# An encoder block: the attention's small sums moved from VectorE to GpSimd, and five orders changed

## The chip, the cores and the metric

One core of a Trainium2 chip runs the whole program in one launch. The metric is device time in microseconds, from a median over several executions. The engines are named as in the profile: PE (TensorE), DVE (VectorE), ACT (ScalarE), POOL (GpSimd) and SP, which only issues transfers.

## The reference, cut to what matters

An encoder layer on 1024 rows of 1024 columns, fp32: sliding-window attention and a two-way retention side by side, a cross-attention into 256 memory tokens, and a SwiGLU. Each ends in a normed addition to the stream. The part at which most of the change is made:

```
blk = jnp.arange(nb)[:, None, None]
...
valid = (jnp.abs(qpos - kpos) <= WINDOW) & (kpos >= 0) & (kpos < S)
s = jnp.where(valid, s, -jnp.inf)
sk = sink.astype(jnp.float32).reshape(ATTN_KV_HEADS, G)[None, :, :, None, None, None]
m = jnp.maximum(jnp.max(s, axis=-1, keepdims=True), sk)
p = jnp.exp(s - m)
p = p / (jnp.sum(p, axis=-1, keepdims=True) + jnp.exp(sk - m))
o = jnp.einsum('bhgnqk,bnkhd->bnqhgd', p.astype(v.dtype), vw)
```

So each row of scores has a maximum that takes in a learned sink logit, and a denominator that is the row's sum plus the sink's exponential.

## The kernel before, in words

Every engine has one instruction stream, written out by hand in its order; semaphores carry the dependencies. An engine does its instructions strictly in that order: one that waits holds up all behind it.

**Matrix products.** Each fp32 factor is split into a high and a low part, and `three()` (L1377 to L1379) does three matmuls for one product. For a weight piece of 128x512, SP loads it into one of four raw slots (`load`: it waits until the low part of the piece four places before is done), ACT rounds the high part, POOL subtracts for the low part, and PE multiplies. Low parts of activations are made by DVE from PSUM. Some products are done by a scheme of seven block products for eight; it needs sums of weight blocks. For the output projection, POOL makes these sums (L1156 to L1161, four rounds of four, 128x512 each) in the attention stage; SP loads a round's blocks, and stores the sums to a scratch in HBM.

**Attention, 248 to 341 us.** 16 steps, two (one per key/value head, four query heads each) for each of the 8 row blocks; I call the two a pair. In step s PE turns the exponentials (L1368), ACT and DVE copy them out (`copy_probs`, L2276 and L3190), and PE does the scores of step s + 2 (L1551) and the values of step s (L1589). DVE does `maxima(s + 2)`: four times the masking and the maximum (L3177), then the addition of the sink to the negated maxima (L3182, 128x4, both inputs in SBUF). ACT does the exponentials of step s + 1 and then the sink's (`sink_term`). In each second step DVE does `denominators(n)`: row sums plus sink exponentials (L3199, 128x8) and the reciprocal (L3201); then `values_out(n)`, which copies the turned values from PSUM (L3208, named junk_c) for PE to turn back. `attended(n)` (L3214) scales them by the reciprocal a step later. POOL's 16 sums for the output projection lie here, each round as soon as its blocks have landed.

**Cross-attention, about 500 to 760 us.** `quarter(q)` on PE is a quarter of the cross-attention's output product; its first begins when DVE has made eight low parts (L3551, semaphore `x_lo`). On ACT `q_round(n)` rounds the query's weight pieces, and `xo_round(n)` the output's 32 pieces; the last of these are mixed with the norms (`post(t)`, `pre(t)`) and with the high parts of turned rows (`row_high(t)`). POOL's low parts are L1255 and L1262.

**SwiGLU, from about 748 us.** `first_chunk(n)` is a product of the first block, four times three matmuls; behind each of the first four PE turns a row block (`turn_rows_h3`, eight transpositions), ACT rounds it (L2716) and DVE makes its low part (L3609). For the later blocks, c = 1 and on, ACT's loop mixes `weight_high(c + 1, j)` (rounding of the next block's weights, which POOL's weight sums L1284 precede), `gate_silu` and `bank_copy` (L2817).

Of the kernel before, what the change touches and what calls it, by code (L numbers as in the profile page):

```python
# [19 lines left out]
ALU = mybir.AluOpType  # L20
# [6 lines left out]
NT = S // P  # L27
# [205 lines left out]
def build(nc, x, mem, norm_mix_pre, norm_mix_post, w_in, attn_sink, attn_out_norm, ret_decay_fwd,  # L233
# [3 lines left out]
    with ExitStack() as ctx:  # L237
# [857 lines left out]
        def _(pool):  # L1095
# [54 lines left out]

            for k in range(RING):
                split(U_O, U_O, k, 512)
            for r in range(RING):
                a11, a12, a21, a22 = (o_stage(r, b) for b in range(4))
                pool.wait_ge(o_in[r % 2], O_IN + 64 * (r // 2 + 1))
                nc.gpsimd.tensor_tensor(a21, a21, a22, ALU.add).then_inc(o_summed, 1)  # L1156
                pool.wait_ge(o_summed, O_SUMMED + 4 * r + 1)
                nc.gpsimd.tensor_tensor(a11, a21, a11, ALU.subtract).then_inc(o_summed, 1)
                pool.wait_ge(o_summed, O_SUMMED + 4 * r + 2)
                nc.gpsimd.tensor_tensor(a12, a12, a11, ALU.subtract).then_inc(o_summed, 1)  # L1160
                nc.gpsimd.tensor_tensor(a22, a22, a11, ALU.subtract).then_inc(o_summed, 1)  # L1161

            pool.wait_ge(dk_v, 12)
            pool.wait_ge(sc_ready, NT * AH)
# [201 lines left out]
        def _(pe):  # L1366
# [581 lines left out]
            def quarter(q):  # L1948

                u = U_XO + q * NK  # L1950
                for k in range(NK):
                    if q == 2 and k >= RING:
                        turn_rows_h3(k - RING)
                    if q == 0 and k in (3, 4):
                        mem_turn(3 + k)
                    pe.wait_ge(w_split, u + k + 1)
                    for t in range(4):
                        if q == 1 and k == 0:
                            pe.wait_ge(x_lo, NK + RING + t + 1)
                        if q == 2 and k == 0:  # L1960
                            pe.wait_ge(xo_gain, t + 1)
                        c = slice((4 * (q // 2) + t) * P, (4 * (q // 2) + t + 1) * P)
                        last = three(ps[:, 4 * (q % 2) + t, :], t_hi[:, k, c], t_lo[:, k, c],
                                     w_hi[:, k % RING, :], w_lo[:, k % RING, :], k == 0, k == NK - 1)
                        if t == 3:
                            last.then_inc(w_used, 1)
                        elif k == NK - 1:
                            last.then_inc(tile_done, 1)

            pe.wait_ge(x_lo, NK)  # L1970
            pe.wait_ge(x_exp, XH * NT)
            quarter(0)
            mem_values(1)
# [4 lines left out]
            def first_chunk(n):  # L1978

                m, bank_no, first, high, low, c = (  # L1980
                    (0, 0, True, t_hi, t_lo, 0), (1, 0, False, t_hi, t_lo, 0), (2, 1, True, t_hi, t_lo, 0),
                    (3, 1, False, t_hi, t_lo, 0), (0, 2, True, t_hi, t_lo, 512), (2, 0, True, t_hi, t_lo, 512),
                    (1, 2, False, t_hi, t_lo, 512), (3, 0, False, t_hi, t_lo, 512))[n]
                if n < 4:
                    pe.wait_ge(g_lo, n + 1)
                if n == 0:
                    pe.wait_ge(h_dve, 8)
                    pe.wait_ge(xo_gain, 12)
                if n == 4:
                    pe.wait_ge(h_dve, 15)  # L1990
                if n == 5:
                    pe.wait_ge(c_act, 1)
                if n == 6:
                    pe.wait_ge(h_dve, 16)
                w_high, w_low = first_weights(m)
                for k in range(4):
                    w = slice(k * P, (k + 1) * P)
                    kk = 4 * (m % 2) + k
                    last = three(ps[:, bank_no, :], w_high[:, w], w_low[:, w], high[:, kk, c:c + 512], low[:, kk, c:c + 512],
                                 first and k == 0, not first and k == 3)  # L2000
                last.then_inc(g_prod, 1)
# [28 lines left out]
                                 first and k == 0, k == 3, not first)  # L2030
                last.then_inc(g_prod, 1)

            for n in range(4):
                first_chunk(n)
                turn_rows_h3(4 + n)
            first_chunk(4)
            for n in range(5, 8):
                first_chunk(n)
# [55 lines left out]
        def _(act):  # L2094
# [431 lines left out]
            for c in range(4):  # L2526
                if c == 2:
                    for i in range(4):
                        act.wait_ge(turned, TURNED_K + i + 1)
                        nc.scalar.activation(kM[:, 2 * i:2 * i + 2, :], bank(4 + i).rearrange("p (k m) -> p k m", k=2),  # L2530
                                             ACT.Copy).then_inc(act_ev, 1)
                    round_units(RING)
                if c == 3:
                    for n in range(3):
                        q_round(n)
                if c == 0:
                    act.wait_ge(o_joined, 12)
                for t in range(NM):
                    if t == 0:
                        act.wait_ge(tile_done, TILES["kv"] + c + 1)  # L2540
                    else:
                        act.wait_ge(w_used, U_KV + NK * (c + 1))
                    dst = kst if c < 2 else vM_hi
                    nc.scalar.activation(dst[:, t, (c % 2) * 512:(c % 2 + 1) * 512], bank(2 * (c % 2) + t),
                                         ACT.Copy).then_inc(act_ev, 1)
                if c == 3:
                    q_round(3)
                if c < 3:
                    for t in (2 * c, 2 * c + 1):
                        hi_parts(h2_turned(t), t_hi, t * P)  # L2550
                if c == 0:
                    round_units(2)
                    sums(("post", 4))
                    round_units(2)
                    sums(("post", 5))
                    round_units(RING)
                elif c == 1:
                    sums(("pre", 4), ("pre", 5), ("post", 6), ("post", 7))
                elif c == 2:
                    round_units(3)  # L2560
                    sums(("pre", 6))
                    round_units(1)
                    sums(("pre", 7))
                else:
                    round_units(RING)
# [210 lines left out]
            post(2)  # L2776
            pre(1)
            xo_round(21)
            post(3)
            pre(2)  # L2780
            xo_round(22)
            row_high(0)
            pre(3)
            xo_round(23)
            row_high(1)
            xo_round(24)
            xo_round(25)
            row_high(2)
            for n in range(26, 32):
                xo_round(n)  # L2790
            row_high(3)
            for t in range(4, NT):
# [56 lines left out]
            for c in range(1, NC - 1):  # L2849
                if c > 1:  # L2850
                    bank_copy(c, 1)
                    weight_high(c + 1, 0)
                weight_high(c + 1, 1)
                bank_copy(c, 2)
                if c == 1:
                    sum_high(6)
                    sum_high(7)
                if c > 1:
                    weight_high(c + 1, 2)
                gate_silu(c, 0)  # L2860
                bank_copy(c, 4)
                if c == 1:
                    weight_high(c + 1, 2)
                weight_high(c + 1, 3)
                weight_high(c + 1, 4)
                weight_high(c + 1, 5)
                gate_silu(c, 1)
                weight_high(c + 1, 6)
# [107 lines left out]
        def _(dve):  # L2976
# [190 lines left out]
            def maxima(s):  # L3167
# [3 lines left out]
                for j in range(G):  # L3171
# [3 lines left out]
                    if s >= 2:  # L3175
# [1 line left out]
                    nc.vector.tensor_tensor_reduce(sm[:, s % 2, j, 0:nk], bank(j, nk), band[:, off:off + nk],  # L3177
                                                   -A_SCALE, nsink[:, h:h + 1], ALU.add, ALU.min,
                                                   wnm[:, n, h:h + 1]).then_inc(w_max, 1)
                dve.wait_ge(w_max, G * (s + 1))  # L3180
                hs = slice(g * G, (g + 1) * G)
                nc.vector.tensor_tensor(wds[:, n, hs], sink[:, hs], wnm[:, n, hs], ALU.add).then_inc(w_small, 1)  # L3182

            def copy_probs(s, j):
                q = G * s + j
# [9 lines left out]
            dve.wait_ge(sink_turned, 1)  # L3195
            def denominators(n):

                dve.wait_ge(w_exp, 10 * (n + 1))
                nc.vector.tensor_tensor(wden[:, n, :], wrs[:, n, :], wes[:, n, :], ALU.add).then_inc(w_den, 1)  # L3199
                dve.wait_ge(w_den, 2 * n + 2)  # L3200
                nc.vector.reciprocal(wrd[:, n, :], wden[:, n, :]).then_inc(w_den, 1)  # L3201

# [20 lines left out]
            for s in range(steps):  # L3223
                n = s // AKV
                copy_probs(s, 1)
                copy_probs(s, 3)
                if s % AKV == 0 and n:
                    attended(n - 1)
                if s + 2 < steps:
                    maxima(s + 2)  # L3230
                if s % AKV == AKV - 1:
                    denominators(n)
                    values_out(n)

            def decay_scores(h):
                for b in range(2):
# [630 lines left out]
```

## Time and profile before

| what | value |
|---|---|
| median of 3 runs | 1394.73 us (1394.01 to 1396.04) |
| profiled execution, its own time | 1395.81 us |
| its span, first to last instruction | 1393.3 us |
| PE busy | 1366.7 us, 98% |
| POOL busy, DVE busy, ACT busy | 876.7, 879.2, 671.6 us |
| mean granted clock of PE | 0.999 |

The profiled execution is one of several. Its span leaves out 2.5 us before the first and behind the last instruction. PE is the engine with hardly any idle time, 27 us in all, so an edit's worth is read from what PE waits for.

### The profile page before, as it was taken

How to read it: one execution, taken by the hardware profiler on the slowest of the kernel's cores; microseconds unless marked ns; L12 is line 12 of the kernel's file. 1: busy time of each engine (PE TensorE's matmuls, PEld its weight loads, DVE VectorE, ACT ScalarE, POOL GpSimd, SP SyncE). 2: the span in 40 equal slices, each digit the busy share in tenths (PEclk: the TensorE clock that was granted, in tenths of full speed). 3: DMA queues.
4: the chain of work that ended last, by engine and by line, in shares of the span. 5: the costliest groups of instructions: out<-in, count | busy, mean ns of one | idle time of the engine just before them, and what ended most of it. 6: DMA issues, size and time to landing. Idle time of an engine off the chain costs nothing.

```text
span 1393.3 us, 18814 instructions
## 1 busy us (share of the span) xinstructions
PE 1366.7 (98%) x6644; PEld 1135.0 (81%) x6644; DVE 879.2 (63%) x1254; ACT 671.6 (48%) x1357; POOL 876.7 (63%) x600
## 2 busy tenths in 40 slices
PE   7999999999999999999999999999999999999998
PEld 7998888756988888888878888888888888878886
DVE  5799997887887888764267732333332333474868
ACT  6432233666686774354376433333333333544454
POOL 1697256421868976511354787777777774799653
PEclk9999999999999999999999999999999999999999
DMA  5676133540027555301535233233333325933354
GB/s 204 211 246 212 46 91 106 159 145 1 1 61 278 176 184 167 102 31 33 187 101 209 62 114 106 98 114 114 106 106 104 100 84 178 370 93 99 110 206 153
DMA packets 137756, 183.56 MB, mean 132 GB/s; under 512 B 10304, under 2 KB 82368, under 8 KB 137664
## 3 DMA queue, kind: packets, MB, share of 16 engines
q1 hardware_dynamic: 135360, 177.25, 38.8%
q10 hardware_dynamic: 2304, 5.13, 1.0%
q8 instruction: 53, 0.87, 0.3%
q14 instruction: 39, 0.32, 0.1%
HBM read 136.98 MB, written 45.35 MB: 131 GB/s over the span
## 4 chain that ended last, share of the span: by engine, by line
PE 82%; DVE 7%; ACT 4%; POOL 4%; issue 2%; DMA 1%; DVEq 0%; SPq 0%; ACTq 0%; POOLq 0%
PE ps L1377 24%; PE ps L1379 24%; PE ps L1378 24%; PE ps L1368 4%; PE ps L1891 2%; POOL w_lo L1246 1%; PE ps L1551 1%; DMA raw<-in_xa_wkv_dram 1%; PE ps L1589 1%; PE ps L1643 1%; DVE x L3775 1%; ACT tables L2098 1%; DVE sm L3177 1%; DVE yf L3768 1%; POOL t_lo L1246 1%
## 5 line engine op out<-in xcount | busy, mean ns | idle before, releaser
L1377 PE MATMUL ps<-w_hi,t_hi 128*128 128x512 f32 (+2 forms) x576 | 219.5, 381 | 4.1 <-DVE t_lo L2990 1.5
L1379 PE MATMUL ps<-w_hi,t_lo 128*128 128x512 f32 (+2 forms) x576 | 217.5, 378 | 0.0
L1378 PE MATMUL ps<-w_lo,t_hi 128*128 128x512 f32 (+2 forms) x576 | 217.4, 377 | 0.0
L1138 POOL TENSOR_TENSOR w_lo<-raw,w_hi 128x512 fp32r<-128x512 f32 (+1 forms) x52 | 82.9, 1600 | 95.5 <-ACT w_hi L2151 95.4
L1377 PEld LDWEIGHTS ps<-w_hi,t_hi 128*128 128x128 f32 x576 | 108.2, 188 | 23.6 <-issue 2.1
L1379 PEld LDWEIGHTS ps<-w_hi,t_lo 128*128 128x128 f32 x576 | 108.1, 188 | 17.6
L1378 PEld LDWEIGHTS ps<-w_lo,t_hi 128*128 128x128 f32 x576 | 108.2, 188 | 17.0
L1262 POOL TENSOR_TENSOR w_lo<-raw,w_hi 128x512 fp32r<-128x512 f32 x32 | 41.0, 1290 | 100.1 <-ACT w_hi L2628 100.1
L3677 DVE TENSOR_TENSOR ev<-ps,ev 128x512 f32<-128x512 f32 x21 | 14.5, 691 | 137.2 <-PE ps L1379 137.2
L2817 ACT ACTIVATE ev<-ps 128x512 f32<-128x512 f32 x63 | 37.5, 595 | 87.7 <-PE ps L1379 87.7
L2151 ACT ACTIVATE w_hi<-raw 128x512 fp32r<-128x512 f32 (+1 forms) x52 | 31.4, 615 | 97.0 <-PE ps L1379 96.7
L2762 ACT ACTIVATE ws<-tables 128x512 fp32r<-128x512 f32 x42 | 26.4, 632 | 106.6 <-POOL tables L1284 106.6
L3677 DVE TENSOR_TENSOR gate<-ps,ev 128x512 f32<-128x512 f32 x42 | 28.9, 687 | 73.4 <-PE ps L1379 73.4
L1292 POOL TENSOR_TENSOR ws<-tables,ws 128x512 fp32r<-128x512 f32 x42 | 54.3, 1293 | 31.5 <-ACT ws L2762 31.5
L1377 PE MATMUL ps<-t_hi,wa 128*128 128x512 f32 x184 | 71.8, 390 | 1.0 <-DVE t_lo L3609 1.0
L1292 POOL TENSOR_TENSOR ws<-gain_b,ws 128x512 fp32r<-128x512 f32 x42 | 54.0, 1288 | 28.5 <-ACT ws L2762 28.5
L1379 PE MATMUL ps<-t_hi,wa 128*128 128x512 f32 x184 | 71.6, 389 | 0.0
L1378 PE MATMUL ps<-t_lo,wa 128*128 128x512 f32 x184 | 71.6, 389 | 0.0
L3719 DVE TENSOR_TENSOR left_a<-gain_b,left_a 128x512 fp32r<-128x512 f32 x39 | 42.0, 1079 | 38.5 <-ACT left_a L2877 38.2
L1377 PE MATMUL ps<-t_hi,ws 128*128 128x512 f32 x168 | 65.5, 390 | 0.6 <-ACT ev L2817 0.6
L1377 PE MATMUL ps<-tok_t,ws 128*128 128x512 f32 x168 | 65.5, 390 | 0.1
L1379 PE MATMUL ps<-t_hi,ws 128*128 128x512 f32 x168 | 65.4, 389 | 0.0
(391 smaller groups left out, 4131.7 us busy)
## 6 DMA issues: line engine op xcount, KB each, us to landing
raw_a<-in_ffn_w_gu_dram SPq DMA_DIRECT2D x44, 256.0 KB, 3.2
raw_b<-in_ffn_w_gu_dram SPq DMA_DIRECT2D x44, 256.0 KB, 3.2
f_rows<-fs SPq DMA_DIRECT2D x44, 256.0 KB, 3.6
gain_b<-f_rows SPq DMA_DIRECT2D x39, 256.0 KB, 2.7
tables<-f_rows SPq DMA_DIRECT2D x38, 256.0 KB, 2.7
f_rows<-fa SPq DMA_DIRECT2D x33, 256.0 KB, 3.4
raw<-in_xa_wo_dram SPq DMA_DIRECT2D x32, 256.0 KB, 2.6
wd_rest<-in_ffn_w_down_dram SPq DMA_DIRECT2D x15, 512.0 KB, 6.3
```

The lines of the kernel that those rows point to most:

```text
L1138: nc.gpsimd.tensor_tensor(w_lo[:, k, 0:width], raw[:, k, 0:width], w_hi[:, k, 0:width].bitcast(F32), ALU.subtract).then_inc(w_split, 1)
L1246: nc.gpsimd.tensor_tensor(lo[:, k, :], memory_raw(n), hi[:, k, :].bitcast(F32), ALU.subtract).then_inc(w_split, kv_covers(n))
L1262: nc.gpsimd.tensor_tensor(lo[:, n % RING, :], raw[:, n % RING, :], hi[:, n % RING, :].bitcast(F32), ALU.subtract).then_inc(w_split, 1)
L1292: nc.gpsimd.tensor_tensor(lo, src, hi.bitcast(F32), ALU.subtract).then_inc(g_lo, 1)
L1368: return nc.tensor.transpose(ps[:, b, col:col + P], src, ident[:, :])
L1377: nc.tensor.matmul(out, a_hi, b_hi, start=start, stop=False, skip_group_check=onto)
L1378: nc.tensor.matmul(out, a_hi, b_lo, start=False, stop=False, skip_group_check=onto)
L1379: return nc.tensor.matmul(out, a_lo, b_hi, start=False, stop=stop, skip_group_check=onto)
L2151: nc.scalar.activation(w_hi[:, s, 0:c1 - c0], raw[:, s, 0:c1 - c0], ACT.Copy).then_inc(w_rounded, 1)
L2817: nc.scalar.activation(dst, bank(3 * (c % 2) + src_bank), ACT.Copy).then_inc(c_act, 1)
L3677: nc.vector.tensor_tensor(dst, bank(3 * (c % 2) + bank_no), other, ALU.add).then_inc(c_dve, 1)
L3719: nc.vector.tensor_tensor(lo, left_raw(u), hi.bitcast(F32), ALU.subtract).then_inc(left_lo, 1)
```

## The change

Six places are edited. A: the sink additions and denominator sums are made by POOL, with one of its 16 weight sums behind each step's; DVE copies the values out before it takes the reciprocal. B: PE waits for the query tile's low parts one tile at a time in `quarter(0)`. C: the turn of row 7 goes from behind `first_chunk(3)` into it, between its second and third group. D: ACT's `q_round(2)` goes behind the copies of the last value tiles. E: `xo_round(22)` and those behind it go one place forward. F: in block c = 2 ACT's `weight_high(3, 2)` goes behind the SiLU and the bank copy.

```diff
 (A, POOL)
-            for r in range(RING):
+            def with_sink(s):
+                n, g = divmod(s, AKV)
+                pool.wait_ge(w_max, G * (s + 1))
+                hs = slice(g * G, (g + 1) * G)
+                nc.gpsimd.tensor_tensor(wds[:, n, hs], sink[:, hs], wnm[:, n, hs], ALU.add).then_inc(w_small, 1)
+            def denominator_sum(n):
+                pool.wait_ge(w_exp, 10 * (n + 1))
+                if n:
+                    pool.wait_ge(w_den, 2 * n + 1)
+                nc.gpsimd.tensor_tensor(wden[:, n, :], wrs[:, n, :], wes[:, n, :], ALU.add).then_inc(w_den, 1)
+            def out_sum(r, step):
                 a11, a12, a21, a22 = (o_stage(r, b) for b in range(4))
-                pool.wait_ge(o_in[r % 2], O_IN + 64 * (r // 2 + 1))
...
+                if step == 0:
+                    pool.wait_ge(o_in[r % 2], O_IN + 64 * (r // 2 + 1))
+                    nc.gpsimd.tensor_tensor(a21, a21, a22, ALU.add).then_inc(o_summed, 1)
...
+            pool.wait_ge(w_den, 1)
+            pool.wait_ge(sink_turned, 1)
+            with_sink(0)
+            with_sink(1)
+            for s in range(NT * AKV):
+                if s + 2 < NT * AKV:
+                    with_sink(s + 2)
+                if s % AKV == AKV - 1:
+                    denominator_sum(s // AKV)
+                out_sum(s // 4, s % 4)
 (A, DVE: maxima, denominators, the loop)
-                dve.wait_ge(w_max, G * (s + 1))
-                hs = slice(g * G, (g + 1) * G)
-                nc.vector.tensor_tensor(wds[:, n, hs], sink[:, hs], wnm[:, n, hs], ALU.add).then_inc(w_small, 1)
-                dve.wait_ge(w_exp, 10 * (n + 1))
-                nc.vector.tensor_tensor(wden[:, n, :], wrs[:, n, :], wes[:, n, :], ALU.add).then_inc(w_den, 1)
                 if s % AKV == AKV - 1:
+                    values_out(n)
+                if s % AKV == AKV - 1:
                     denominators(n)
-                    values_out(n)
 (B, PE)
+                        if q == 0 and k == 0:
+                            pe.wait_ge(x_lo, (1, 1, NK - 1, NK)[t])
-            pe.wait_ge(x_lo, NK)
 (C, PE)
                 for k in range(4):
+                    if n == 3 and k == 2:
+                        turn_rows_h3(7)
-            for n in range(4):
+            for n in range(3):
                 first_chunk(n)
                 turn_rows_h3(4 + n)
+            first_chunk(3)
 (D, ACT)
-                    for n in range(3):
+                    for n in range(2):
                         q_round(n)
...
                 if c == 3:
+                    q_round(2)
                     q_round(3)
 (E, ACT)
             xo_round(21)
+            xo_round(22)
             post(3)
             pre(2)
-            xo_round(22)
+            xo_round(23)
             row_high(0)
             pre(3)
-            xo_round(23)
+            xo_round(24)
             row_high(1)
-            xo_round(24)
             xo_round(25)
+            xo_round(26)
             row_high(2)
-            for n in range(26, 32):
+            for n in range(27, 32):
                 xo_round(n)
 (F, ACT)
-                if c > 1:
+                if c > 2:
                     weight_high(c + 1, 2)
                 gate_silu(c, 0)
                 bank_copy(c, 4)
-                if c == 1:
+                if c <= 2:
                     weight_high(c + 1, 2)
```

## Rows read from the trace of the kernel before

**Rows 1.** The page, busy time of each engine over the span

```profile
PE 1366.7 (98%) x6644; PEld 1135.0 (81%) x6644; DVE 879.2 (63%) x1254; ACT 671.6 (48%) x1357; POOL 876.7 (63%) x600
```

**Rows 2.** What PE waited for: us in total, times, longest

```profile
PE ps L1368 <- DVE junk_c L3208: 4.4, 7, 1.7
...
PE ps L1377 <- DVE t_lo L3609: 1.0, 1, 1.0
...
PE ps L1377 <- POOL w_lo L1262: 0.9, 2, 0.6
...
PE ps L1377 <- DVE t_lo L3551: 0.3, 1, 0.3
```

**Rows 3.** Timeline of PE about 808 us: start, us, engine, line, [idle before]

```profile
807.88 0.39 PE L1378 MATMUL ps<-tok_t,ws 128*128 128x512 f32 x1
808.11 0.39 PE L1379 MATMUL ps<-tok_t,ws 128*128 128x512 f32 x1
809.05 0.47 PE L1377 MATMUL ps<-t_hi,ws 128*128 128x512 f32 x1 [0.55 <-ACT ev L2817]
809.36 0.39 PE L1378 MATMUL ps<-t_lo,ws 128*128 128x512 f32 x1
```

**Rows 4.** Timeline of PE, transpositions of the attention's values

```profile
284.53 0.66 PE L1368 MATMUL ps<-ident,junk_c 128*128 128x128 f32 x4 [1.01 <-DVE junk_c L3208]
...
295.14 0.66 PE L1368 MATMUL ps<-ident,junk_c 128*128 128x128 f32 x4 [0.95 <-DVE junk_c L3208]
...
314.81 0.66 PE L1368 MATMUL ps<-ident,junk_c 128*128 128x128 f32 x4 [0.18 <-DVE junk_c L3208]
...
324.64 0.66 PE L1368 MATMUL ps<-ident,junk_c 128*128 128x128 f32 x4 [0.18 <-DVE junk_c L3208]
```

**Rows 5.** Timeline of DVE in the attention, a disturbed and a quiet pair

```profile
282.61 1.00 DVE L3182 TENSOR_TENSOR wmx<-sink,wnm 128x4 f32<-128x4 f32 x1
...
283.72 0.20 DVE L3201 RECIPROCAL wrd<-wrs 128x8 f32<-128x8 f32 x1
...
323.54 0.16 DVE L3182 TENSOR_TENSOR wmx<-sink,wnm 128x4 f32<-128x4 f32 x1
...
323.93 0.65 DVE L3208 COPY junk_c<-ps 128x512 f32<-128x512 f32 x1
...
325.66 0.56 DVE L3190 COPY pTw<-ps 128x384 f32<-128x384 f32 x1 [0.61 <-PE ps L1368]
```

**Rows 6.** Timeline of POOL in the attention

```profile
271.66 1.26 POOL L1161 TENSOR_TENSOR z<-z 128x512 f32<-128x512 f32 x1
...
283.67 1.27 POOL L1160 TENSOR_TENSOR z<-z 128x512 f32<-128x512 f32 x1
...
290.20 1.27 POOL L1156 TENSOR_TENSOR z<-z 128x512 f32<-128x512 f32 x1 [4.03 <-DMA z<-in_w_out_dram]
```

**Rows 7.** POOL by line and form, 256 to 345 us

```profile
L1156 POOL TENSOR_TENSOR z<-z 128x512 f32<-128x512 f32 x4 | 5.1, 1278 | 23.1 <-DMA z<-in_w_out_dram 23.1
...
L1168 POOL TENSOR_TENSOR rqT<-rqT,qtab 128x1024 f32<-128x1024 f32 x1 | 2.4, 2363 | 0.0
```

**Rows 8.** Timeline of DVE about 760 us

```profile
759.96 0.69 DVE L3619 TENSOR_TENSOR y<-ps,y 128x512 f32<-128x512 f32 x1
...
763.22 1.29 DVE L3609 TENSOR_TENSOR t_lo<-ps,t_hi 128x512 fp32r<-128x512 f32 x2 [1.37 <-ACT t_hi L2716]
```

**Rows 9.** Timeline of PE, the turn of row 7

```profile
761.95 1.04 PE L1368 MATMUL ps<-ident,y 128*128 128x128 f32 x8
```

**Rows 10.** Timeline of POOL about 725 us

```profile
723.08 5.05 POOL L1262 TENSOR_TENSOR w_lo<-raw,w_hi 128x512 fp32r<-128x512 f32 x4 [0.45 <-ACT w_hi L2628]
...
728.56 2.52 POOL L1262 TENSOR_TENSOR w_lo<-raw,w_hi 128x512 fp32r<-128x512 f32 x2 [0.43 <-ACT w_hi L2628]
```

**Rows 11.** Timeline of ACT, at the places of the last two edits

```profile
727.85 0.63 ACT L2628 ACTIVATE w_hi<-raw 128x512 fp32r<-128x512 f32 x1 [1.62 <-DMA raw<-in_xa_wo_dram]
...
807.27 0.63 ACT L2762 ACTIVATE ws<-gain_b 128x512 fp32r<-128x512 f32 x1 [3.58 <-POOL gain_b L1284]
```

More of the change, by code:

```diff
@@ L1152, in _ @@
                 split(U_O, U_O, k, 512)
-            for r in range(RING):
-                a11, a12, a21, a22 = (o_stage(r, b) for b in range(4))
-                pool.wait_ge(o_in[r % 2], O_IN + 64 * (r // 2 + 1))
[L1156 to L1161, printed above, removed]
+            def with_sink(s):
[3 more added lines that the diff above has]
+                nc.gpsimd.tensor_tensor(wds[:, n, hs], sink[:, hs], wnm[:, n, hs], ALU.add).then_inc(w_small, 1)
@@ new lines, in denominator_sum @@
+            def denominator_sum(n):
[4 more added lines that the diff above has]
+            def out_sum(r, step):
+                a11, a12, a21, a22 = (o_stage(r, b) for b in range(4))
+                if step == 0:
+                    pool.wait_ge(o_in[r % 2], O_IN + 64 * (r // 2 + 1))
+                    nc.gpsimd.tensor_tensor(a21, a21, a22, ALU.add).then_inc(o_summed, 1)
+                elif step == 1:
+                    pool.wait_ge(o_summed, O_SUMMED + 4 * r + 1)
+                    nc.gpsimd.tensor_tensor(a11, a21, a11, ALU.subtract).then_inc(o_summed, 1)
+                elif step == 2:
+                    pool.wait_ge(o_summed, O_SUMMED + 4 * r + 2)
+                    nc.gpsimd.tensor_tensor(a12, a12, a11, ALU.subtract).then_inc(o_summed, 1)
+                else:
+                    nc.gpsimd.tensor_tensor(a22, a22, a11, ALU.subtract).then_inc(o_summed, 1)
```

## The prediction

> **What bounds the kernel now.** I read the page's busy line first: PE is busy for 98% of the span [rows 1], so what any edit can give is at most PE's 27 us of idleness, and only where PE itself waits. The view of PE's waits says what they are [rows 2]. Four of its groups lie where the diff works: 4.4 us in seven waits for DVE's copy of the attention values (L3208), 1.0 for DVE's low part of a turned row (L3609), 0.9 for POOL's low parts of the cross-attention's output weights (L1262, two waits), and 0.3 for DVE's low part of the first query tile (L3551). A fifth, 0.55 us for ACT's bank copy (L2817), stands in [rows 3].
>
> Those figures are idle time, and idle time is not the whole loss. In [rows 3] matmuls start every 0.23 us (807.88, 808.11). The one that waited starts 0.94 behind its predecessor, and the next 0.31 behind that one. Lost against 0.23 each: 0.71 + 0.08 = 0.79 us, where the view says 0.55. The reason is that a busy interval of 0.39 overlaps the next by 0.16, and the pipe refills after a wait. So I add 0.16 to each wait between matmuls of this shape, and 0.08 to 0.11 of refill.
>
> In the attention the loop period shows it. PE's transposition of the values comes once per pair of steps: 284.53 to 295.14 is 10.61 us, 314.81 to 324.64 is 9.83 [rows 4]. The idle times differ by 0.77, the periods by 0.78. What differs is seen on DVE [rows 5] and POOL [rows 6]. The sink addition L3182, over 128x4 elements, takes 1.00 us at 282.61 and ends at 283.61, just before POOL begins its next instruction (283.67). At 323.54, with POOL idle, it takes 0.16. It stands directly ahead of the denominators and of the copy for which PE waits, so POOL's sums hold that copy back. The reciprocal at 283.72 runs wholly inside POOL's instruction of 283.67 to 284.94 and takes 0.20: not every DVE instruction is held.
>
> **Part A, the attention.** Removed from DVE per pair: two sink additions, one denominator sum; and the reciprocal goes behind the copy. In the quiet pair that starts the copy 323.93 - 323.54 = 0.39 us earlier [rows 5]; in the disturbed ones 0.84 more. PE waits 0.95 there, and 0.18 in the quiet pairs [rows 4]: both are covered, the quiet ones with little to spare (the wait and its 0.16 of lost overlap make 0.34). The whole loss is 4.42 + 7 x 0.16 = 5.5 us. The margin of 0.05 in the four quiet pairs is thin, so I leave 0.1 in each: **A = 5.1**, with 3.0 (the four small ones stay, and one large one half) and 5.5 as ends.
>
> Added to POOL: 24 small additions, of which no row exists. POOL's 128x512 takes 1.28 and its 128x1024 2.36 [rows 7]; a line through both leaves 0.19 us at no columns, so 0.2 for 8 columns (an estimate); ends 0.16 (what DVE takes) and 1.28. Call T the end of DVE's last maximum. POOL sees it at about T + 0.1, does the sink addition and the denominator sum by T + 0.5; DVE copies until T + 0.65 and then takes the reciprocal: nothing waits. Behind the reciprocal DVE's queue holds the copies of the probabilities, with 0.61 us of idle time for PE between two of them [rows 5]. With PE 0.34 earlier and the copy 0.39 earlier, the sum may come as late as about T + 1.05 before DVE is late for PE. ACT's sink exponential comes behind four exponentials of its step, so it has more room.
>
> Moved: a weight sum of 1.28 us per step, queued on POOL behind the small additions. A step lasts 4.9 us, so POOL is idle again before the next maxima. But its first sum of each four waits for a DMA, and the next sink additions are queued behind it. Before, a round's stores and the load into their place took from 271.66 + 1.26 to 290.20 = 17.3 us [rows 6]. Now a round's last sum is followed, five steps later, by the round that needs this load: 5 x 4.9 - 1.3 = 23 us. It fits with 6 to spare. SP's queue holds the output projection's other weight loads behind the last store, so these start later too, by most of the attention's second half; PE's retention work lies between them and their use. I cost that at nothing; if the cover were too short, PE would wait for output weights at the projection's start.
>
> First I weigh the lock. The rows say that L3182, both inputs in SBUF, is held, and that the reciprocal is not. The Trainium skill, "SBUF — State Buffer", section "Who interferes with whom", says the same of the port pair that VectorE and GpSimd share: an exclusive lock for a whole instruction, taken by a VectorE instruction with two SBUF inputs against a GpSimd one that reads SBUF, and by its 2-port modes. If L3177, which reads a table and a per-partition scalar from SBUF beside PSUM, counted as two, then by that rule the sums, spread over all steps, would hold the maxima as they held the additions.
>
> **Part B** lets PE start the query quarter before DVE's eighth low part. Only the fourth tile needs it, 9 matmuls x 0.23 = 2.1 us later; 0.3 + 0.16 + 0.1 of the wait goes: **B = 0.55**, ends 0.3 and 0.55.
>
> **Part C** sends the eight transpositions of row 7 ahead of six matmuls, 6 x 0.23 = 1.4 us. The chain behind them (ACT rounds, DVE subtracts at 763.22 after 1.37 idle for ACT [rows 8]) then ends 1.4 earlier, and PE waited 1.0. DVE's row sum that the second half needs ended at 759.96 + 0.69 = 760.65 [rows 8], before PE comes to that half: its turn of 761.95 begins at 760.57 and takes 1.04 [rows 9]. **C = 1.0 + 0.16 + 0.1 = 1.25**, ends 0.9 and 1.25.
>
> **Part D** moves one rounding of a query weight on ACT behind two copies. POOL, which takes the rounded piece next, has two earlier pieces before it at about 1.3 each [rows 7], against two copies of about 0.5: hidden. If POOL had already done them, PE would wait some tenths; the copies gain as much. **D = 0**, ends -0.3 and +0.3.
>
> **Part E** rounds cross-attention output pieces 22 and on one place earlier. The last two pieces are late because each load follows the low part four pieces before: POOL's four from 723.08 [rows 10] free the first slot at 724.35, ACT gets piece 30 at 727.85 after 1.62 idle for the DMA [rows 11], POOL takes both from 728.56 on [rows 10], and PE waits twice. With piece 26 beside 25, its low part ends about 1.7 us earlier and that of 27 1.3; the DMA's 3.5 stays. Piece 30 is then out of the way, piece 31 just (0.1 to spare). The loss now is 0.9 + 2 x 0.16 + 2 x 0.11 = 1.4: **E = 1.3**, ends 0.4 and 1.4.
>
> **Part F** puts ACT's rounding, which waited 3.58 us for POOL until 807.27 [rows 11], behind the SiLU and the bank copy. Those start earlier by at least the rounding's place on ACT, 0.63 less some overlap, and by more if the gate was joined before; PE's idle time is 0.55. The rounding then comes later by the two it lets past, about 1 us, and POOL's work on the piece with it, but that weight is for the next block's third product, several products of 12 matmuls (2.8 us) away. **F = 0.8** [rows 3], ends 0.4 and 0.8.
>
> **The sum**: 5.1 + 0.55 + 1.25 + 0 + 1.3 + 0.8 = **9.0 us**. The profiled execution took 1395.81 (span 1393.3 and 2.5 around it), so 1386.8 by its own scale. It stands 1.1 above the median of 1394.73; on the median's scale 1385.7. What stands behind the attention follows PE or loads that follow PE's use, so I let the gains add up.
>
> **Rivals.** (1) *Part of it only*: idle time alone comes back, or the quiet pairs keep their waits, or piece 31 is late. By the low ends the sum is 3.0 + 0.3 + 0.9 - 0.3 + 0.4 + 0.4 = 4.7: about 1390.0. For it: three margins of 0.1 or less. (2) *A gives nothing*, since the lock passes to another DVE instruction such as the maxima; B to F alone give 3.9: 1390.8. With half an instruction (0.6 us) lost in each of the 16 steps PE would lose 9.6 in place of 5.5, and with B to F it would be no change. Against it: the reciprocal's 0.20. (3) *Slower*: POOL's small additions are dear. With x each, the denominators come at T + 0.1 + 2x, DVE's queue stands behind the reciprocal, and PE loses 8 x (2x - 0.95) us in place of 5.5. A gives nothing from x = 0.82; all edits together nothing from 1.07; slower by 0.2% from 1.24; at 1.28 PE loses 12.9: 12.9 - 5.5 - 3.9 = +3.5, 1398.2. Against it: the line of [rows 7]. The Trainium skill, "GPSIMD Engine Reference", section "4.1 Engine selection", would leave such additions on VectorE, GpSimd being about twice as slow with two inputs; by that x is 0.32, an estimate, and the sum the same.
>
> **How the numbers follow.** 0.2% or 2.8 us is about what this measurement can tell from no change. My forecast (7 to 10 us) 0.60; rival 1 0.24; rival 2 0.08, of which half within 0.2%; rival 3 0.08, of which 0.03 slower, 0.03 within, 0.02 faster. Faster 0.60 + 0.24 + 0.04 + 0.02 = 0.90, same 0.07, slower 0.03. Range: 1383.8 (all upper ends, 9.6, and the medians' spread) to 1390.5.
>
> **What would show it.** Right: PE's waits for L3208, L3609, L1262, L2817 and L3551 gone; pair periods near 9.5 all along; no sink addition on DVE; POOL's small additions near 0.2. Wrong: a DVE wait for POOL ahead of the reciprocal, maxima longer than 0.6, a POOL wait for a DMA in the middle of the steps, or a PE wait for L1262 that stays.

## The result, and the profile after

The changed kernel took 1386.8 us (median, 1385.56 to 1387.6) against 1395.38 for the kernel before on the same chip: ratio 0.9939, 95% interval 0.9924 to 0.9954, so 8.5 us faster, with 6.4 to 10.6 as the interval's ends. The forecast was 9.0 us, which on the scale of the medians stood for 1385.7. Its profiled execution has a span of 1384.9 us, 8.4 shorter.

The page of the kernel after, its busy line:

```profile
PE 1364.0 (98%) x6644; PEld 1136.0 (82%) x6644; DVE 878.7 (63%) x1230; ACT 671.2 (48%) x1357; POOL 882.7 (64%) x624
```

PE still is the bound [rows 1]. What PE waited for, after:

```profile
PE ps L1407 <- issue: 1.7, 1, 1.7
PE ps L1407 <- POOL w_lo L1276: 1.1, 1, 1.1
PE ps L1407 <- DVE tok_t L3668: 1.0, 1, 1.0
...
PE ps L1407 <- DVE y L3345: 0.4, 1, 0.4
```

Here L1407 is the L1377 of before, and other line numbers have moved likewise. None of the four groups of [rows 2] is left, nor the wait for the bank copy in [rows 3]. Two are new: 1.0 us for DVE's token sums (tok_t, L3668), in the second SwiGLU block, and 0.2 for POOL's low part of a cross-attention weight (L1285). The 1.7 us of "issue" is a wait near 1229 us for which the profile shows no cause; the last experiment finds it. PE's transposition of the values in the attention, after:

```profile
291.28 0.60 PE L1398 MATMUL ps<-ident,junk_c 128*128 128x128 f32 x4
...
300.72 0.60 PE L1398 MATMUL ps<-ident,junk_c 128*128 128x128 f32 x4
...
310.16 0.60 PE L1398 MATMUL ps<-ident,junk_c 128*128 128x128 f32 x4
```

The pair now takes 9.44 us all along, where it took 10.61 and 9.83 [rows 4], and no wait stands in these rows. DVE and then POOL, after:

```profile
318.73 0.68 DVE L3239 COPY junk_c<-ps 128x512 f32<-128x512 f32 x1
...
319.33 0.19 DVE L3232 RECIPROCAL wrd<-wrs 128x8 f32<-128x8 f32 x1
```

```profile
318.89 0.20 POOL L1158 TENSOR_TENSOR wmx<-sink,wnm 128x4 f32<-128x4 f32 x1 [2.96 <-DVE wnm L3213]
319.04 0.20 POOL L1165 TENSOR_TENSOR wrs<-wrs,wes 128x8 f32<-128x8 f32 x1
319.20 1.28 POOL L1180 TENSOR_TENSOR z<-z 128x512 f32<-128x512 f32 x1
```

The copy (318.73) follows the last maximum at once. Beside it POOL does the sink addition and the denominator sum and begins a weight sum, and the reciprocal (319.33) follows the copy without a wait. All 24 small additions take what the estimate said, 0.2 us:

```profile
L1158 POOL TENSOR_TENSOR wmx<-sink,wnm 128x4 f32<-128x4 f32 x16 | 3.2, 199 | 56.1 <-DVE wnm L3213 56.1
...
L1165 POOL TENSOR_TENSOR wrs<-wrs,wes 128x8 f32<-128x8 f32 x8 | 1.6, 203 | 0.5 <-ACT wes L2301 0.5
```

PE does the same 6644 matmuls in both kernels, so the two traces can be laid against each other matmul by matmul (part C's eight apart). What an edit gives or takes in the difference of these starts I call its worth in starts. Where the difference changes (at times of the kernel before):

| place | change, us | forecast |
|---|---|---|
| attention, 264 to 334 us (A) | -5.36 | -5.1 |
| 445 us, PE's wait for L3313 (L3345 after) | -0.57 | none |
| 518 us, wait for L1246 and what follows (D) | +0.02 | 0 |
| 643 us (B) | -0.56 | -0.55 |
| 730 to 732 us (E) | -1.41 | -1.3 |
| 762 to 765 us (C) | -1.29 | -1.25 |
| 786 us, new wait for L3668 | +0.85 | none |
| 809 us (F) | -0.83 | -0.8 |
| 1238 us, a wait of both kernels, 1.2 then 1.7 | +0.49 | none |
| the rest | +0.20 | |
| sum | -8.46 | -9.0 |

### The profile page after: what moved, and what is told of

Same layout as the page of the kernel before. It is cut to its first block, busy times and chain, and to the rows that moved or that the text cites. A ratio compares the mean times of both kernels' runs of the same rounds, so it can differ in the third digit from the quotient of the medians.

```text
span 1384.9 us, 18822 instructions
## 1 busy us (share of the span) xinstructions
PE 1364.0 (98%) x6644; PEld 1136.0 (82%) x6644; DVE 878.7 (63%) x1230; ACT 671.2 (48%) x1357; POOL 882.7 (64%) x624
## 4 chain that ended last, share of the span: by engine, by line
PE 80%; DVE 8%; ACT 4%; POOL 3%; issue 2%; DMA 2%; SPq 0%; DVEq 0%; ACTq 0%; POOLq 0%
PE ps L1407 23%; PE ps L1409 23%; PE ps L1408 23%; PE ps L1398 4%; PE ps L1921 2%; PE ps L1619 1%; PE ps L1581 1%; POOL w_lo L1276 1%; DMA raw<-in_xa_wkv_dram 1%; PE ps L1673 1%; ACT tables L2132 1%; DVE x L3807 1%; DMA raw<-o_sums 1%; DVE left_a L3751 1%; DVE yf L3800 1%
## 5 line engine op out<-in xcount | busy, mean ns | idle before, releaser
L1407 PE MATMUL ps<-w_hi,t_hi 128*128 128x512 f32 (+2 forms) x576 | 219.4, 381 | 2.2 <-DVE t_lo L3026 1.2
L1407 PEld LDWEIGHTS ps<-w_hi,t_hi 128*128 128x128 f32 x576 | 108.2, 188 | 20.3 <-DVE t_lo L3026 1.6
L1407 PE MATMUL ps<-t_hi,wa 128*128 128x512 f32 x184 | 71.7, 390 | 0.0
L1407 PE MATMUL ps<-tok_t,ws 128*128 128x512 f32 x168 | 65.5, 390 | 1.0 <-DVE tok_t L3668 1.0
L1407 PE MATMUL ps<-t_hi,ws 128*128 128x512 f32 x168 | 65.4, 390 | 0.1
L1409 PE MATMUL ps<-tok_t,ws 128*128 128x512 f32 x168 | 65.4, 389 | 0.0
L1408 PE MATMUL ps<-tok_t,ws 128*128 128x512 f32 x168 | 65.4, 389 | 0.0
```

The costliest lines, as they stand in the source:

```text
L1407: nc.tensor.matmul(out, a_hi, b_hi, start=start, stop=False, skip_group_check=onto)
L1408: nc.tensor.matmul(out, a_hi, b_lo, start=False, stop=False, skip_group_check=onto)
L1409: return nc.tensor.matmul(out, a_lo, b_hi, start=False, stop=stop, skip_group_check=onto)
```

## The experiments

Each ran beside the kernel before on the same chip; ratios are to that.

**Part A alone** (the POOL and DVE hunks of A, on the kernel before).

```diff
...
+            for s in range(NT * AKV):
+                if s + 2 < NT * AKV:
+                    with_sink(s + 2)
...
```

> Part A alone on the kernel before. Sum of terms: the seven waits for the copy of the values go, 5.4 us of PE starts between 264 and 335 us, and nothing of the rest: the waits for the low parts of row 7 (1.0), the output weights (0.9), the bank copy (0.55) and the query tile (0.3) stay. About 1389.5, ratio 0.996. Rival, later work takes the attention's gain back: less than 3 us at the end though the attention is 5.4 shorter.

1389.32 us, ratio 0.9959 (0.9946 to 0.9971): 5.7 us. PE's starts gain 5.4 in the attention, as reckoned, and keep them: the difference at the end of the trace is 6.9, of which 0.8 lies at the wait near 1238 us and 0.35 near 730, where PE waited less in this execution though no edit touches the places. The rival falls.

**Parts B to F alone** (A undone).

> The changed kernel with part A undone (B to F alone). Sum of terms: B 0.56, C 1.3, E 1.4, F 0.8, less 0.85 for the new wait behind DVE's token sums: 3.2 us faster than before, about 1391.8, ratio 0.9977. The attention is as before, with waits of 1.7, 1.0, 0.95 and four of 0.18. Rival, the new wait comes from A's earlier start and not from C: it is absent here, 4.1 us faster.

1390.57, ratio 0.9964 (0.9951 to 0.9978): 5.0 us, more than the sum's 3.2. The new wait is there (0.9), so A doesn't cause it. Most of the surplus stands in places the edits don't touch: 1.7 us in starts in the attention and 0.7 near 1238 us. In this execution PE waited only 2.7 us for the copy of the values. POOL's sums begin when their blocks land (the third round at 279.20, in the profile of before at 280.96), and this time they held only one of the sink additions that stand ahead of the copy for about 1 us, not three. By the ratios A is worth 0.9964 - 0.9939, or 3.5 us, beside B to F, and 5.7 alone; the intervals are wide enough for both to be 4.5, so no difference between the two is shown.

**Part C undone.**

```diff
-                    if n == 3 and k == 2:
-                        turn_rows_h3(7)
...
-            for n in range(3):
+            for n in range(4):
                 first_chunk(n)
                 turn_rows_h3(4 + n)
-            first_chunk(3)
```

> The changed kernel with part C undone. Theory: C gives 1.3 us and then, since it moves DVE ahead of POOL's weight work, costs 0.85 where POOL's low part and DVE's token sums now hold each other up. So without C the wait for row 7's low part is back (1.0 idle, 1.25 in starts), the one for the token sums (0.95 idle) is gone, and the sum is only 0.4 us slower than the changed kernel. Rival, any earlier arrival of PE makes that wait: it stays, and the kernel is 1.3 us slower.

1386.93, ratio 0.994 (0.9927 to 0.9952): as the changed kernel. PE's wait for row 7's low part is back at 1.0, the one for the token sums is gone. In starts, leaving C out costs 1.2 at row 7 and gives 0.8 back at the token sums. That the two medians are equal is partly chance: the wait of both kernels near 1230 us was 0.2 there (1.7 in the changed kernel), 1.0 less in starts, and PE waited 0.8 more near 440. **Part C alone:**

> Part C alone on the kernel before. Theory: C by itself brings about the collision of POOL's low part with DVE's token sums: the wait for row 7's low part goes (1.25 us), the two token sums take over 2 us each in place of 1.2, and PE waits 0.9 for them: net 0.4 us, the same as before by the medians. Rival, the collision needs the other edits too: net 1.2 us, no wait for the token sums.

1394.65, ratio 0.9998 (0.9989 to 1.0008): as before, and PE waits 1.0 for the token sums. In starts C gives 1.3 at row 7 and loses 0.9 here, so the rival falls. The same DVE pair in the kernel without C, with C alone, and in the changed kernel, with POOL beside it there (timelines; x2 is two subtractions of 128x1024):

```profile
776.20 2.36 DVE L3665 TENSOR_TENSOR tok_t<-y,tok_t 128x1024 fp32r<-128x1024 f32 x2 [0.67 <-ACT tok_t L2776]
```

```profile
782.50 4.46 DVE L3639 TENSOR_TENSOR tok_t<-y,tok_t 128x1024 fp32r<-128x1024 f32 x2 [0.66 <-ACT tok_t L2747]
```

```profile
773.35 4.46 DVE L3668 TENSOR_TENSOR tok_t<-y,tok_t 128x1024 fp32r<-128x1024 f32 x2 [0.67 <-ACT tok_t L2779]
```

```profile
771.17 2.07 POOL L1314 TENSOR_TENSOR gain_b<-gain_b,raw_a 128x512 f32<-128x512 f32 x1 [0.17 <-POOL gain_b L1314]
773.21 1.30 POOL L1322 TENSOR_TENSOR wa<-raw_a,wa 128x512 fp32r<-128x512 f32 x1
774.87 1.87 POOL L1322 TENSOR_TENSOR wa<-raw_a,wa 128x512 fp32r<-128x512 f32 x1 [0.36 <-ACT wa L2797]
```

Without C the pair takes 2.36. In the changed kernel it comes 0.14 us behind POOL's low part of 773.21 and is held to its end, and its second half by the one of 774.87. With C alone it is the same 4.46. In the kernel before, DVE's chain and POOL's weight work met at another phase, and the pair (783.58) took 2.36. So C by itself brings the collision about, and the 0.85 us that it costs.

**POOL's weight sums later** (on the changed kernel). The two sums for block 2 stand ahead of POOL's low parts; here they go behind two of them.

```diff
-            weight_sum_of(2, 1)
-            weight_sum_of(2, 2)
             for c in range(2, NC):
                 weight_low(c, 0)
                 if c > 2:
                     weight_sum_of(c, 1)
                 weight_low(c, 1)
-                if c > 2:
-                    weight_sum_of(c, 2)
+                if c == 2:
+                    weight_sum_of(c, 1)
+                weight_sum_of(c, 2)
```

> The changed kernel with POOL's two weight sums for block 2 put behind its two low parts of that block. Theory (the lock): DVE's two token sums, 2.2 and 2.3 us in the changed kernel, take 1.2 each, PE's wait of 0.95 for them goes, about 0.9 us faster than the changed kernel. Rival, PE is simply ahead of a chain of DVE work that is as long without POOL: the wait stays at 0.9 whatever POOL does; or the sums come too late for ACT's rounding of block 2's third weight and a new wait of about 1 us takes its place.

1385.0, ratio 0.9926 (0.9913 to 0.9938). DVE's chain there:

```profile
769.41 1.21 DVE L3661 TENSOR_TENSOR t_sum<-y 128x1024 f32<-128x1024 f32 x1
...
771.89 2.36 DVE L3667 TENSOR_TENSOR tok_t<-y,tok_t 128x1024 fp32r<-128x1024 f32 x2 [0.67 <-ACT tok_t L2778]
...
775.53 4.46 DVE L3667 TENSOR_TENSOR tok_t<-t_sum,tok_t 128x1024 fp32r<-128x1024 f32 x2 [0.68 <-ACT tok_t L2778]
```

The first pair takes 2.36 again and PE's wait is gone; the next pair (775.53) now is the one held, and PE doesn't need it yet. In starts it is 1.6 us against the changed kernel, more than the 0.9, since smaller waits behind that one went too. No work was saved, only put at another time.

**The swap alone** (on the kernel before).

```diff
                 if s % AKV == AKV - 1:
-                    denominators(n)
                     values_out(n)
+                    denominators(n)
```

> The kernel before with one swap alone: DVE copies the values out before it adds the denominators and takes the reciprocal; sink additions and denominators stay on DVE, POOL's sums stay in blocks. Theory (two causes, order and lock): the copy comes 0.3 us earlier, so the four waits of 0.18 go (1.4 us of starts) and the three large ones shrink by 0.3 each: about 2.3 us, 1393.0. The sink additions still take about 1 us beside POOL's sums. Rival, the lock is all: the large waits stay as they are, under 1.5 us.

1393.06, ratio 0.999 (0.9981 to 0.9999): 1.4 us; 2.6 in the starts of the attention. Its PE rows:

```profile
273.55 0.66 PE L1368 MATMUL ps<-ident,junk_c 128*128 128x128 f32 x4 [1.19 <-DVE junk_c L3208]
...
283.17 0.66 PE L1368 MATMUL ps<-ident,junk_c 128*128 128x128 f32 x4
...
293.77 0.66 PE L1368 MATMUL ps<-ident,junk_c 128*128 128x128 f32 x4 [0.88 <-DVE junk_c L3208]
...
303.33 0.66 PE L1368 MATMUL ps<-ident,junk_c 128*128 128x128 f32 x4
```

The quiet pairs lose their wait (9.56 us). Where the sink addition is held (1.02 and 1.14 us on DVE here) PE waits 1.19 and 0.88. Order and lock are two causes, as the theory says. In this execution the pair at 283 was not hit, and some 1.0 of the 2.6 stands there, not all of it the swap's.

**The swap and the sums spread, small additions left on DVE.**

```diff
...
+            for s in range(NT * AKV):
+                pool.wait_ge(w_small, min(s + 3, NT * AKV))
+                out_sum(s // 4, s % 4)
...
```

> The kernel before with the swap and with POOL's sums spread, one per step, each behind DVE's sink addition; nothing small moves to POOL. Theory of the lock: no sink addition is held (0.16 all along), but the denominator sum, both inputs in SBUF, now comes while POOL's sum runs and is held to its end: about 1 us instead of 0.16, and the reciprocal and the copies of the probabilities with it. By the slack of T + 1.05 from the prediction PE would lose up to 0.6 per pair, so A's gain shrinks from 5.3 to 1 to 3 us. Rival, the spreading and the order alone are worth all of A: 5.3 us, the move to POOL nothing.

1392.8, ratio 0.9988 (0.9979 to 0.9997): 1.7 us; 3.1 in the attention's starts. DVE by line and form, in this kernel:

```profile
L3208 DVE TENSOR_TENSOR wrs<-wrs,wes 128x8 f32<-128x8 f32 x8 | 6.1, 760 | 0.0
L3191 DVE TENSOR_TENSOR wmx<-sink,wnm 128x4 f32<-128x4 f32 x16 | 2.6, 162 | 0.6
```

The sink additions are free (162 ns), but now seven of the eight denominator sums are held (760 ns on average where it took 160). The pair takes 9.76 (301.88 to 311.63 and 321.39 in its timeline). The rival falls: spreading and order without the move to POOL give 3.1 of A's 5.4 us in starts, and 1.7 of 5.7 by the ratios.

**The denominator sum behind the weight sum** (on part A alone).

```diff
-                if s % AKV == AKV - 1:
-                    denominator_sum(s // AKV)
                 out_sum(s // 4, s % 4)
+                if s % AKV == AKV - 1:
+                    denominator_sum(s // AKV)
```

> Part A with one swap on POOL: the denominator sum behind the step's weight sum and not ahead of it, so that it comes about 1.3 us later, near T + 1.8. By the prediction's slack of T + 1.05 PE would lose 0.7 us in each of 8 pairs, 5.8 us, and A would give nothing. Rival, the slack is longer (PE needs the copies later than reckoned): 2 us or less are lost against part A alone.

1393.56, ratio 0.9991 (0.9983 to 1.0). POOL, DVE, and PE's rows:

```profile
311.24 0.20 POOL L1158 TENSOR_TENSOR wmx<-sink,wnm 128x4 f32<-128x4 f32 x1 [2.88 <-DVE wnm L3206]
311.39 1.27 POOL L1175 TENSOR_TENSOR z<-z 128x512 f32<-128x512 f32 x1
312.62 0.20 POOL L1165 TENSOR_TENSOR wrs<-wrs,wes 128x8 f32<-128x8 f32 x1
```

```profile
311.08 0.68 DVE L3232 COPY junk_c<-ps 128x512 f32<-128x512 f32 x1
312.86 0.20 DVE L3225 RECIPROCAL wrd<-wrs 128x8 f32<-128x8 f32 x1 [1.09 <-POOL wrs L1165]
```

```profile
302.11 0.60 PE L1397 MATMUL ps<-ident,junk_c 128*128 128x128 f32 x4
304.86 1.52 PE L1618 MATMUL ps<-pTw,z 128*64 128x256 f32 x12 [0.33 <-DVE z L3238]
...
311.95 0.60 PE L1397 MATMUL ps<-ident,junk_c 128*128 128x128 f32 x4
```

The reciprocal waits 1.09 us for POOL; DVE's queue stands, and PE waits 0.33 for the scaled values (L3238) of the pair before. The pair takes 9.84 in place of 9.44: 0.4 lost, not 0.7 (T is 311.16 and the sum came at T + 1.66, so PE would begin to wait at about T + 1.27, an estimate from these rows). Against part A alone about 3 us are lost in the attention's starts, 4.5 by the ratios, whose intervals allow 2 to 7. Neither the 5.8 nor the 2 was right; the mechanism of rival 3 is there, with its threshold 0.2 us later.

**The sums in blocks, small additions on POOL** (on part A alone).

```diff
-                out_sum(s // 4, s % 4)
+                for r in {0: (0, 1), 4: (2,), 6: (3,)}.get(s, ()):
+                    for step in range(4):
+                        out_sum(r, step)
```

> Part A with POOL's sums left in blocks of four (rounds 0 and 1 behind step 0, round 2 behind step 4, round 3 behind step 6) while the small additions are on POOL. Theory of the queue: the sink addition of step 3 stands behind 10 us of sums, ACT's sink exponential and the exponentials of step 4 behind it, and PE loses about 5 us there, some more where rounds 2 and 3 wait for their load: A's gain is gone, within 3 us of before either way. Rival, the small additions have room enough: as part A alone, 5 to 6 us faster.

1398.7, ratio 1.0033 (1.0022 to 1.0045): 4.6 us slower than before. POOL, ACT and PE there:

```profile
277.00 1.26 POOL L1180 TENSOR_TENSOR z<-z 128x512 f32<-128x512 f32 x1
278.22 0.20 POOL L1158 TENSOR_TENSOR wmx<-sink,wnm 128x4 f32<-128x4 f32 x1
```

```profile
278.46 0.20 ACT L2298 ACTIVATE wes<-wmx 128x4 f32<-128x4 f32 x1 [3.50 <-POOL wmx L1158]
```

```profile
280.46 1.98 PE L1620 MATMUL ps<-pTw,z 128*64 128x256 f32 x8 [5.80 <-DVE z L3240]
```

The sink addition of step 3 stands behind eight sums, ACT's sink exponential waits 3.50 for it, and PE 5.80. Rounds 2 and 3 cost nothing. So without the spreading, at least with the blocks at these places, the move costs more than it gives. Against part A alone 7.8 us are lost in the attention's starts: 5.9 at this wait, and the other 2.0 behind it, where PE's clock was lower (last section).

**The changed kernel again, and part D undone.**

> The changed kernel once more, as a yardstick on this chip: 8 to 9 us faster than before, with the wait for the token sums (0.95) and the one near 1229 us (1.7) again, since both come from the order of the work, and with the waits near 440 and 513 us different, since these hang on when transfers land.

> The changed kernel with part D undone. In runs without D PE waited 0.4 to 0.9 us for DVE's low part of the value tiles (near 519 us) wherever the key/value weight before it landed early. Theory: D is worth that, so this kernel shows that wait or, where the weight lands late, a wait of about 1 us for the weight in its place; median 0 to 0.9 us slower than the changed kernel. Rival, the prediction's D = 0: the same with and without, in whichever of the two ways the weight lands.

1386.73, ratio 0.994 (0.9928 to 0.9953), and 1387.64, ratio 0.9947 (0.9933 to 0.996); the intervals overlap, so the times don't tell the two apart. The changed kernel shows the waits for the token sums (1.0) and near 1229 us (1.9) again. The waits tell more of D. In the profiles of seven of the eight kernels without D PE waited for DVE's value tiles (vM_lo), 0.4 to 2.4 us; in none of the six with D. Three of the seven, part A alone, part D undone and part C alone:

```profile
PE ps L1407 <- DVE vM_lo L3455: 0.9, 1, 0.9
```

```profile
PE ps L1407 <- POOL w_lo L1276: 1.0, 1, 1.0
...
PE ps L1407 <- DVE vM_lo L3460: 0.6, 1, 0.6
```

```profile
PE ps L1377 <- DVE vM_lo L3432: 2.4, 1, 2.4
```

Undoing D cost 0.9 us in starts at that place, though the key/value weight (L1276) was late too, in the same kernel. The eighth, the profiled execution of before, had only the late weight (0.9).

**Two low parts of the down projection ahead.** The wait near 1229 us was left, so I looked at POOL's queue: the low part (1227.31 in the changed kernel) whose rounding ACT had begun at 1219.88 stood behind three sums, all held by DVE's two-input subtractions at 1.7 each, where such a sum alone takes 1.28 [rows 7]. On the changed kernel, with the edit of the weight sums, and:

```diff
             for g in range(NG + 1):
-                if g < NG:
-                    right_low(NG + g)
+                right_low(NG + g)
...
+            right_low(2 * NG + 1)
             for g in range(NG):
...
-                right_low(2 * NG + g)
+                if g > 1:
+                    right_low(2 * NG + g)
```

> The changed kernel with the two weight sums of block 2 put back, as in the run before, and with POOL's first two low parts of the down projection's third product ahead of its last first sum and of two second sums. Theory: the wait of 1.7 us near 1229 is POOL's, whose low part stood 6.8 us behind its rounding because of three sums that DVE's subtractions held at 1.74 each; moved ahead it is in time, and up to 1.2 us of the 1.9 in starts come back, the rest going into a wait for the third unit: about 1384.0, 10 to 12 us faster than before. Rival, the sums behind are late by as much: the wait moves to the third unit and nothing is gained on 1385.0.

1384.08, ratio 0.9922 (0.9908 to 0.9935): 10.9 us faster than before, the lowest median of all. The interval overlaps that of the weight sums alone (0.9913 to 0.9938), so what these two low parts give is read from the starts. ACT, DVE and POOL in the changed kernel, then POOL in this one:

```profile
1219.88 0.62 ACT L2939 ACTIVATE right_b<-x 128x512 fp32r<-128x512 f32 x1
...
1221.01 3.47 DVE L3751 TENSOR_TENSOR left_b<-tables,left_b 128x512 fp32r<-128x512 f32 x2
...
1222.20 3.44 POOL L1368 TENSOR_TENSOR wd<-wd_rest,wd 128x512 f32<-128x512 f32 x2
1225.61 1.74 POOL L1378 TENSOR_TENSOR x<-wd_rest,wd 128x512 f32<-128x512 f32 x1
1227.31 1.71 POOL L1359 TENSOR_TENSOR right_b<-x,right_b 128x512 fp32r<-128x512 f32 x1
```

```profile
1220.93 1.74 POOL L1358 TENSOR_TENSOR right_b<-x,right_b 128x512 fp32r<-128x512 f32 x1
...
1224.33 1.73 POOL L1358 TENSOR_TENSOR right_b<-x,right_b 128x512 fp32r<-128x512 f32 x1
```

The low part ends at 1222.67 and PE begins the product at 1225.99 without a wait; 1.85 us in starts came back there, and no wait took its place at the third unit. So the rival falls, and the wait near 1229 us was one for POOL's low part. Over the whole trace 1.2 us are left against the weight sums alone.

## Why the prediction was right, and where it was not

**Bound and price of a wait.** Pricing a wait by the starts behind it was right. The seven attention waits were 4.42 idle and gave 5.36; B, C, E and F, 0.29 + 0.97 + 0.88 + 0.55 = 2.7 idle, gave 4.09 (0.56 + 1.29 + 1.41 + 0.83), with 3.9 forecast. The sum of idle times would have been 7.1. These parts together gave 9.45, and the table's other rows took 1.0 back, so that 8.5 lies so near 9.0 is in part luck. It is chance, too, that the measured median equals the 1386.8 of the prediction, which went by the profiled execution's scale. The upper ends of the range add up to 9.8, and not to 9.6.

**A** was right in size and cause: 5.36 against 5.1, and swap and lock are separate, shown by the swap alone and by the spread sums. But that size belongs to one execution: how often POOL's sums hit a sink addition hangs on when their blocks land, and 2.7 or 2.8 us of wait stood in two others with the same attention (parts B to F alone, C alone) in place of 4.4. One profile of before doesn't tell how usual 4.4 is, so it is in part luck that 5.1 came out so near.

**The lock** was weighed rightly, and the trace of before could have settled rival 2 (the lock passes to the maxima):

```profile
280.96 1.28 POOL L1156 TENSOR_TENSOR z<-z 128x512 f32<-128x512 f32 x1 [8.04 <-DMA z<-in_w_out_dram]
...
281.41 0.61 DVE L3177 CUSTOM_DVE_ANT_0 sm<-ps,tables,nsink 128x384 f32<-128x384 f32 x1
```

A maximum that runs wholly inside a POOL sum takes 0.61 us, as it does with POOL idle (0.61). In the changed kernel no maximum meets a sum at all: each sum ends before the next step's maxima, so its 0.61 says nothing of the lock. The reciprocal stays at 0.2 beside a sum. By the Trainium skill, "SBUF — State Buffer", section "Who interferes with whom", a VectorE instruction with two SBUF inputs contends with a GpSimd instruction that reads SBUF; the runs agree, with the denominator sum at 760 ns where sums run beside it and the token subtractions at 4.46 for 2.36.

**The step that didn't hold is "I let the gains add up".** C's 1.29 was right, and 0.85 of it went into a collision that C made by shifting DVE against POOL. I had followed C to PE's next need and not to what DVE's earlier chain would run beside.

**D = 0** held between the two profiled executions, since before's shows no wait for the value tiles. There PE waited for a late key/value weight instead. A late weight doesn't always cover D: with D undone in the changed kernel both waits stood, and D was worth 0.9 us in starts. No median shows it.

**Rival 3's** slack, T + 1.05, was 0.2 us too short by the estimate of T + 1.27.

**What stays open:** why the load of the key/value weight and the weights before the wait near 440 us (0.4 to 1.4 in these runs) land when they do. The -0.57 us there in the first profile was not seen again in the second of the same kernel, where PE waited 1.1 us.

## What to carry to other kernels

DVE and POOL hold each other up by phase, so an edit that only moves work earlier can make or undo a collision elsewhere: behind such a gain, look for two-input subtractions of twice their length, and put the work that PE needs later behind what it needs first. Small additions can go to the other engine if they don't queue behind its long work there; spread the long work. Price a wait by starts, and know which waits belong to one execution alone.

## What the hardware showed that I had not expected

A wait can cost PE's clock as well. The granted clock by windows, of the sums in blocks, then of the changed kernel's second profile, then of its first. The last three numbers of a row are the granted clock as a share of 2.4 GHz, the DMA share and GB/s:

```profile
280.00:285.00 5.00, 4.54 (x23) 3.07 (x24) 2.85 (x10) 0.55 (x2) 0.20 (x1) 0.57 0.95 312
285.00:289.00 4.00, 4.00 (x31) 2.35 (x30) 3.54 (x12) 3.15 (x11) 0.36 (x2) 1.00 0.44 140
```

```profile
1229.30:1230.40 1.10, 0.95 (x4) 0.85 (x5) 1.10 (x2) 0.00 (x0) 1.10 (x2) 1.00 0.86 216
1230.40:1232.60 2.20, 2.20 (x7) 1.73 (x7) 1.89 (x4) 0.63 (x1) 2.20 (x3) 0.56 0.48 126
```

```profile
1230.20:1232.40 2.20, 2.19 (x10) 1.54 (x9) 1.76 (x3) 0.63 (x1) 2.20 (x3) 1.00 0.40 119
```

Behind 5.80 us idle PE ran at a mean of 0.57 for 5 us, so mostly at 1.2 GHz, and lost another 2.0 us in starts. Behind 1.86 us idle the clock fell about a microsecond after PE had resumed, to a mean of 0.56 in that window, and PE lost 1.3; behind 1.71 us, at the same place of the same kernel, it stayed at 1.00. Behind C alone's 2.4 us it fell too, to a mean of 0.52 over 3.5 us. In the fourteen profiles the clock is lower at no other place but in the last 4 us, so the waits are the likely cause; why 1.71 us left it alone is not shown. A wait of this length is worth removing for more than itself.
